# Attention scores of three of four attentions in three float32r products instead of one float32 product

## The chip, the core and the metric

The kernel runs on one core of one Trainium2 chip. The metric is the device time of one execution in microseconds (us), from start to end. The engines are called PE (TensorE, matmul), PEld (its weight loads), DVE (VectorE), ACT (ScalarE), POOL (GpSimd) and SP (SyncE).

## What is computed

The reference is a first block (a bidirectional mLSTM with a Fourier branch and a mixture of 16 experts) followed by two attention layers. Each layer has two attentions over 1,024 tokens, so there are four, called A, B, C and D here. The change touches A, B and D. Their scores are the part that matters:

```python
# A: differential attention, 4 heads with two 64-wide halves each
s = jnp.einsum("bqhcd,bkhcd->bhcqk", qb, k) * scale
s = s - (slopes[:, None, None] * dist)[None, :, None]
s = jnp.where(allowed, s, -jnp.inf); p = jax.nn.softmax(s, axis=-1)
w = p[:, :, 0] - lam * p[:, :, 1]
o = jnp.einsum("bhqk,bkhe->bqhe", w, v)       # then an RMS norm per row
# B: forgetting attention, 8 heads of 64, causal
s = jnp.einsum("bqhd,bkhd->bhqk", qb, k) * scale + cq[..., :, None] - cum[:, :, None, :]
# D: 8 heads of 64, each chunk of 64 queries sees 9 chunks of keys
s = jnp.einsum("bnqhd,bnkhd->bnhqk", qc, kb) * scale + bias[None, None]
```

## The kernel before

The program is written by hand in Bass: every engine has its own list of instructions, each runs strictly in the order in which it was written, and semaphores tie the lists together. The second block runs in stages: projections of queries and keys (`qk_pe` and its kin), the projection of the values, the attention, and so on for A, B, gates and output, then C, D, gates and output.

`Attn` holds the plan of an attention. There are 32 pairs of (c, b): c is one of four columns of heads (a head with two halves for A, two heads for the others), b is a block of 128 queries. Within a c the blocks come in the order 7, 0, 6, 1, 5, 2, 4, 3. A pair covers nk blocks of 128 keys; in A and B that is b + 1, so 8, 1, 7, 2, 6, 3, 5, 4, and in D at most 5, so 5, 1, 5, 2, 5, 3, 5, 4. Scores of a pair are made in chunks of up to 512 keys, one or two per pair; each attention has 48 chunks. By width, A and B have 24 of 512, 8 of 384, 8 of 256 and 8 of 128 columns each; D has 20, 4, 4 and 20.

A chunk is two float32 matmuls that contract over 64 rows each: half 0 on rows 0 to 63, half 1 on rows 64 to 127 (line 1591). The trace shows each float32 matmul as two records, so a chunk is four. The stationary operand is the block of queries, the moving one the keys.

All engines go through the same steps i. In step i with pair a = i:
- PE: scores(a, chunk 0), transposes of pair i-3 for half 0, scores(a, chunk 1), the product with the values of pair i-4 (`outputs`), transposes for half 1. Chunk q of the scores waits until DVE has read chunk q-2, since there are two sets of banks.
- DVE: `maxima(a, 0)` (line 2686: adds the bias, finds the row maxima, and moves the scores from PSUM), `weights(i-2)`, `empty(i-3)` (line 2721), `maxima(a, 1)`, `outputs(i-4)` (line 2732 in A, 2735 otherwise), and in A at the end of a column `complete` (lines 2740 and 2742), which waits for ACT's square root.
- ACT: exponentials of pair i-1 for half 0 (line 2078), emptying of the transposes of pair i-3 (line 2090), exponentials for half 1, and in A, one step before DVE's `complete`, `squares(c)` (line 2098 and the root on line 2101). That step is i = 11, 19, 27 and 35.

The biases are strips of 512 KB that POOL loads by DMA into a few regions in turn (`BIAS`, lines 497 to 499 and 1076 to 1086). The load into a region that was used waits until the last column that reads it has been through `maxima`. B has eight strips, one for each head; column c reads strips 2c and 2c+1.

`S` gives a semaphore, `before` the count that earlier stages left on a shared one. `split[...]` are float32r views of the same memory.

Of the kernel before, what the change touches and what calls it, by code (L numbers as in the profile page):

```python
# [53 lines left out]
class Attn:  # L54
# [5 lines left out]
    def __init__(self, p, layer, mix0, span, dv):  # L60
        self.p, self.layer, self.mix0, self.dv = p, layer, mix0, dv
        self.heads = 1 if p == "A" else 2
        blocks = [b for i in range(TT // 2) for b in (TT - 1 - i, i)]
        self.pairs = [(c, b, max(0, b - span), b - max(0, b - span) + 1) for c in range(4) for b in blocks]
        self.n = len(self.pairs)
        self.chunks = [(q[3] + 3) // 4 for q in self.pairs]
        self.chunk0 = [sum(self.chunks[:g]) for g in range(self.n + 1)]
        self.last = {q[0]: g for g, q in enumerate(self.pairs)}
        self.fins = {}
        if p == "A":  # L70
            for c in range(4):
# [8 lines left out]
        self.wide0 = [sum(1 for o in self.order[:i] if wide(o)) for i in range(len(self.order) + 1)]  # L80

    def bias_uses(self, c):
# [14 lines left out]
def build(nc, a, out, scratch):  # L97
# [21 lines left out]
    with ctx:  # L119
# [12 lines left out]
        def before(name):  # L132
# [9 lines left out]
                       for p in ("aq", "ak", "bq", "bk", "cq", "ck", "dq", "dk")])  # L142
# [3 lines left out]
                        ("x2_in", {str(3 + i): 16 for i in range(3)})])  # L146
        share("gpsimd", [("mirror", {"ed": 4}), ("gain", {"ed": TT}), ("r0norm", {"ed": 4}), ("r1norm", {"ed": 16})])
        share("few", [(p, {"_mm": 1}) for p in ("gate", "mid", "dn", "forget")])
        share("dram", [(p, {"_out": 16, "_in": 16}) for p in ("hT", "fu")])
# [7 lines left out]
                            "_pv": at.n, "_o": at.n, "_on": 4 if n == "A" else 0,  # L157
                            **{"A": {"_bias0": 32, "_bias1": 32}, "B": {f"_bias{i}": 32 for i in range(4)},
                               "C": {"_bias0": 16}, "D": {f"_bias{i}": 32 for i in range(4)}}[n]})
                       for n, at in ATT.items()])  # L160

        def sb(name, cols, dt=F32, parts=P):
# [10 lines left out]
                   ("kctx", NH * CTX), ("cols", NCH * 4 * NG),  # L173
                   ("sel_wT", 8 * P), ("lam_f", 448), ("dftc", 2 * P + 1))
        with ExitStack() as views:
            split = {n: views.enter_context(nc.sbuf_tensor(n + "_r", [P, c], F32R)) for n, c in REGIONS}
        ring, hidden, ctx_hidden, pair, wide, small, kctx, cols, sel_wT, lam_f, dftc = (sb(n, c) for n, c in REGIONS)
        ident = sb("ident", P)
# [12 lines left out]
        wrt = sb("wrt", KT * NEXP)  # L191
        extra = sb("extra", SEQ)
        wgate = extra[:, 0:KT * (FROW + NG)]
# [276 lines left out]
        def aff_slot(t):  # L470
# [674 lines left out]
        def _(pe):  # L1145
# [432 lines left out]
            def attn_pe(name):  # L1578
# [3 lines left out]
                def scores(g, j):  # L1582
# [155 lines left out]
        def _(act):  # L1738
# [272 lines left out]
            def qk_act(*keys, then_v=None, norm=None, root=None, stats=None, aside=None, late=None):  # L2011
# [33 lines left out]
                if then_v:  # L2045
                    for t in range(TT):
                        next_job(s2, len(items) + t, every, src)
                        if then_v == "dv" and t == 0:
                            act.wait_ge(S("rC_out"), before("rC_out") + 16)
# [19 lines left out]
            def attn_act(name):  # L2069
# [39 lines left out]
                for i, (a, e, _, t, u, fins) in enumerate(at.steps()):  # L2109
# [124 lines left out]
        def _(dve):  # L2234
# [373 lines left out]
            def qk_dve(*keys, then_v=None, norm=None, norms=None, sums=None, aside=None, late=None):  # L2608
# [33 lines left out]
                if then_v:  # L2642
                    for t in range(TT):
                        next_job(s2, len(items) + t, every, src)
                        if then_v == "dv" and t == 0:
                            dve.wait_ge(S("rC_out"), before("rC_out") + 16)
# [13 lines left out]
            def attn_dve(name):  # L2660
# [94 lines left out]
                for i, (a, _, w, t, u, fins) in enumerate(at.steps()):  # L2755
# [16 lines left out]
                    for c in fins:  # L2772
                        mix(c)

            def gates_dve(layer):
# [198 lines left out]
```

## Time and profile before

| | |
|---|---|
| median of 3 runs | 3056.41 us (3053.8 to 3064.21) |
| span of the profiled execution | 3053.8 us |
| attention A | about 1797 to 1926 us of the span |
| attention B | about 2096 to 2226 us |
| attention D | about 2736 to 2846 us |
| PE busy | 2816.0 us (92%) |
| DVE busy | 1606.6 us (53%) |
| ACT busy | 1331.7 us (44%) |

Busy time is the union of the instructions' spans. Matmuls are pipelined, and their records overlap, so how long a matmul holds PE is read from the distance of two starts and not from a record's own duration. An idle time in square brackets names the engine that ended it.

### The profile page before, as it was taken

The page shows a single profiled execution, that of the slowest core. Times are in us where ns is not written, and L with a number is a line of the kernel's source. Part 1 is how long each engine was busy: PE and PEld are TensorE (multiplying, and loading weights), DVE is VectorE, ACT ScalarE, POOL GpSimd, SP SyncE. Part 2 cuts the span into 40 slices and gives each one's busy share as a digit, 9 for nine tenths or more (in the row PEclk, how much of TensorE's full clock was granted, in tenths as well). Part 3 has the DMA queues.
Part 4 walks back from the last instruction along what each step waited for, and adds up shares of the span by engine and source line. Part 5 has one row for each costly group of instructions (what it writes and reads, how often), then busy time and mean ns, then how long its engine had stood idle before and what let it go on. Part 6 is the DMA issues. An engine that isn't in the chain of part 4 may idle for free. (4 is left out here: it accounts for less than half of the span.)

```text
span 3053.8 us, 37726 instructions
## 1 busy us (share of the span) xinstructions
PE 2816.0 (92%) x13816; PEld 2062.0 (68%) x13830; DVE 1606.6 (53%) x3074; ACT 1331.7 (44%) x2473; POOL 215.5 (7%) x248
## 2 busy tenths in 40 slices
PE   6899999999994899999997998999999989999998
PEld 3457885788783666666665765676677775866676
DVE  1258553344357666666645558554632556536533
ACT  2333253232242555555535537644642548437421
POOL 0000000000000011100005000000020000000500
PEclk9999999999995999999998999999999999999999
DMA  9510020323424799999975300201042201000321
GB/s 363 193 55 28 28 84 1 110 83 110 154 104 179 266 360 362 365 364 363 362 249 142 83 21 8 56 29 42 15 119 75 97 15 57 28 18 19 111 83 55
DMA packets 178377, 401.25 MB, mean 131 GB/s; under 512 B 7948, under 2 KB 9004, under 8 KB 177712
## 3 DMA queue, kind: packets, MB, share of 16 engines
q1 hardware_dynamic: 158224, 329.27, 30.7%
q0 software_dynamic: 19856, 69.92, 7.0%
q8 instruction: 97, 1.59, 0.2%
q14 instruction: 56, 0.46, 0.0%
q10 hardware_dynamic: 144, 0.01, 0.0%
HBM read 363.37 MB, written 35.81 MB: 131 GB/s over the span
## 5 line engine op out<-in xcount | busy, mean ns | idle before, releaser
L778 PE MATMUL psum<-ring_r,kctx_r 128*128 128x512 f32 (+1 forms) x544 | 213.9, 393 | 0.0
L778 PE MATMUL psum<-ring_r,cols_r 128*128 128x512 f32 (+1 forms) x544 | 213.4, 392 | 0.0
L2078 ACT ACTIVATE ring<-ring,att 128x256 f32<-128x256 f32 (+7 forms) x256 | 173.2, 677 | 68.5 <-DVE att L2686 68.5
L1591 PE MATMUL psum<-wide 64*128 64x512 f32 (+2 forms) x704 | 149.7, 505 | 17.1 <-DVE att L2686 14.2
L2549 DVE TENSOR_TENSOR ring_r<-ring,pair_r 128x1024 fp32r<-128x1024 f32 x128 | 148.0, 1218 | 21.6 <-ACT pair_r L1965 21.6
L1462 PE MATMUL psum<-ring_r,wide_r 128*128 128x512 f32 x384 | 150.3, 391 | 0.0
L616 DVE TENSOR_TENSOR ring_r<-ring,ring_r 128x1024 fp32r<-128x1024 f32 x48 | 58.7, 1225 | 129.7 <-ACT ring_r L613 129.3
L1404 PE MATMUL psum<-small_r,ring_r 128*128 128x512 f32 x320 | 125.8, 393 | 0.8 <-DVE pair L2439 0.8
L1406 PE MATMUL psum<-small_r,ring_r 128*128 128x512 f32 x320 | 126.3, 395 | 0.0
L1965 ACT ACTIVATE pair_r<-ring 128x1024 fp32r<-128x1024 f32 x128 | 124.4, 1046 | 0.0
L778 PEld LDWEIGHTS psum<-ring_r,kctx_r 128*128 128x128 f32 x544 | 105.1, 193 | 22.4
L1609 PE MATMUL psum<-ident,ring 128*128 128x128 f32 x640 | 116.9, 291 | 1.6 <-DVE ring L2713 1.6
L778 PEld LDWEIGHTS psum<-ring_r,cols_r 128*128 128x128 f32 x544 | 103.7, 191 | 21.6
L1609 PEld LDWEIGHTS psum<-ident,ring 128*128 128x128 f32 x640 | 67.9, 141 | 73.8 <-issue 40.0
L777 PE MATMUL psum<-small_r,kctx_r 128*128 128x512 f32 (+1 forms) x240 | 100.8, 420 | 18.3 <-DVE sel_wT_r L746 9.0
L300 PE MATMUL psum<-pair,wide 128*128 128x512 f32 x256 | 114.1, 599 | 2.9 <-DMA pair<-in_w_down 2.9
L300 PE MATMUL psum<-hidden,wide 128*128 128x512 f32 x256 | 112.6, 593 | 1.0 <-DVE wide L2560 1.0
L777 PE MATMUL psum<-small_r,cols_r 128*128 128x512 f32 (+1 forms) x240 | 98.7, 411 | 15.4 <-DVE wide_r L746 14.1
L1461 PE MATMUL psum<-pair_r,wide_r 128*128 128x512 f32 x256 | 101.9, 398 | 4.5 <-DVE ring_r L2549 3.1
L1405 PE MATMUL psum<-hidden_r,ring_r 128*128 128x512 f32 x256 | 101.1, 395 | 0.0
L1696 PE MATMUL psum<-wide_r,ring_r 128*128 128x512 f32 x256 | 100.6, 393 | 0.0
L1463 PE MATMUL psum<-pair_r,wide_r 128*128 128x512 f32 x256 | 100.4, 392 | 0.0
(542 smaller groups left out, 6976.3 us busy)
## 6 DMA issues: line engine op xcount, KB each, us to landing
ring<-in_w_gate SPq DMA_DIRECT2D x64, 1024.0 KB, 8.8
ring<-in_w_up SPq DMA_DIRECT2D x32, 1024.0 KB, 9.5
hidden<-in_w_up SPq DMA_DIRECT2D x32, 1024.0 KB, 9.4
hidden<-in_w_down SPq DMA_DIRECT2D x32, 1024.0 KB, 7.2
pair<-in_w_down SPq DMA_DIRECT2D x32, 1024.0 KB, 8.8
ring<-in_w_ada SPq DMA_DIRECT2D x24, 1024.0 KB, 13.1
ring<-in_w_in SPq DMA_DIRECT2D x24, 1024.0 KB, 7.1
ring<-in_even_w_in SPq DMA_DIRECT2D x16, 1024.0 KB, 13.8
```

Of the source, the lines that this page charges most:

```text
L300: mm = pe.matmul(outp, l, r, start=(i == 0), stop=(i == len(pairs) - 1))
L777: self.eng.matmul(outp, XHIGH[b][:, k, :], whigh(key, k)[:, 0:wd], start=(k == 0), stop=False)
L778: self.eng.matmul(outp, XHIGH[b][:, k, :], low[:, k, 0:wd], start=False, stop=False)
L1404: pe.matmul(outp, w, high[:, j, :], start=(j == 0), stop=False)
L1406: mm = pe.matmul(outp, lows[:, k, span(c)], high[:, j, :], start=False, stop=(j == kn - 1))
L1461: pe.matmul(outp, xh[:, k, :], high, start=(k == 0), stop=False)
L1462: pe.matmul(outp, xh[:, k, :], low[:, k, :], start=False, stop=False)
L1591: mm = pe.matmul(bank(2 * (q % 2) + h)[:, 0:n], qT2[row, c, span(b)], kT2[row, 0 if name == "C" else c, k:k + n], start=True, stop=not dia ...
L1609: mm = pe.transpose(turned(i)[:, span(k)], sv[:, span(k)], ident[:])
L1965: act.activation(MHIGH[j % 2][p // 2][:, PK * (p % 2):PK * (p % 2 + 1), :], MRAW[slot][:, ks, :], ACT.Copy).then_inc(S("mw_high"), 1)
L2078: act.activation(sv, sv, ACT.Exp, bias=nmx[:, q:q + 1], scale=-1.0, accum_out=esum[:, r:r + 1]).then_inc(S(name + "_e"), 1)
L2549: dve.tensor_tensor(MLOW[slot][:, ks, :], MRAW[slot][:, ks, :], MHIGH[j % 2][p // 2][:, PK * (p % 2):PK * (p % 2 + 1), :].bitcast(F32), AL ...
```

## The change

For A, B and D each key and query vector is split on chip: ACT copies it, rounded to float32r, to a "high" region (`split_high`), and DVE subtracts the high part from it and writes the remainder over the original, as float32r (`split_low`). The scores become three float32r products in place of one float32 product: high x high, high x low of the keys, low of the queries x high. Each of them is again done on the two row halves. C keeps its float32 product.

Keys are split a column at a time (128x1024). Queries are split a column at a time in A (128x1024) and a block at a time in B and D (128x128). The first ones (`ahead`) are split in the projection of the values, at t = 2. The others are at the end of a step's work, behind everything else of that step: after the pairs 3, 11 and 19 the next column's keys (in A the queries too), and in B and D in each of the first 29 steps the queries of the pair three steps on. On DVE a `split_low` waits for the `split_high` of the same piece. PE waits before a pair's first chunk for its `split_low`.

The region `extra` is now needed for the keys' high part. So B's biases have three regions in turn and not four, and D's third bias region is in `ctx_hidden`.

```diff
+        per = self.n // 4
+        self.ahead = [("k", 0), ("q", 0)] if p == "A" else [("k", 0)] + [("q", g) for g in range(3)]
+        self.splits, self.split_of, made = {}, {}, list(self.ahead)
+        for i in range(self.n):
+            self.splits[i] = [("k", i // per + 1)] if i % per == 3 and i // per < 3 else []
+            if p == "A":
+                self.splits[i] += [("q", c) for _, c in self.splits[i]]
+            elif i + 3 < self.n:
+                self.splits[i].append(("q", i + 3))
...
-        BIAS = {"A": [cols[:, 0:D], extra[:]], "B": [cols[:, 0:D], extra[:], tail, ctx_hidden[:, 0:D]],
+        BIAS = {"A": [cols[:, 0:D], extra[:]], "B": [cols[:, 0:D], tail, ctx_hidden[:, 0:D]],
                 "C": [ctx_hidden[:, i * 256:(i + 1) * 256] for i in range(8)],
-                "D": [cols[:, 0:640], cols[:, 640:1280], extra[:, 0:640], tail[:, 0:640]]}
+                "D": [cols[:, 0:640], cols[:, 640:1280], ctx_hidden[:, 0:640], tail[:, 0:640]]}
...
+        def split_high(act, name, event):
...
+            src, high, _ = halves_of(name, event)
+            act.activation(high, src, ACT.Copy).then_inc(S(name + "_high"), 1)
+
+        def split_low(eng, name, event):
+
+            eng.wait_ge(S(name + "_high"), before(name + "_high") + ATT[name].split_of[event] + 1)
+            src, high, low = halves_of(name, event)
+            eng.tensor_tensor(low, src, high.bitcast(F32), ALU.subtract).then_inc(S(name + "_low"), 1)
...
-                    for h in range(2):
-                        row = slice(HD * h, HD * (h + 1))
-                        mm = pe.matmul(bank(2 * (q % 2) + h)[:, 0:n], qT2[row, c, span(b)], kT2[row, 0 if name == "C" else c, k:k + n],
-                                       start=True, stop=not diagonal, skip_group_check=diagonal)
+                    if name == "C":
+                        factors = [(qT2[:, c, span(b)], kT2[:, 0, k:k + n])]
+                    else:
+                        if j == 0:
+                            pe.wait_ge(S(name + "_low"), before(name + "_low") + at.split_before(g))
+                        qh, kh = QHIGH[name][c % 2][:, span(b)] if name == "A" else QHIGH[name][g % 4], KHIGH[name][c % 2][:, k:k + n]
+                        factors = [(qh, kh), (qh, klow[:, c, k:k + n]), (qlow[:, c, span(b)], kh)]
+                    for f, (qf, kf) in enumerate(factors):
+                        for h in range(2):
...
                     for c in fins:
                         mix(c)
+                    if name != "C" and a is not None:
+                        for event in at.splits[a]:
+                            split_high(act, name, event)
...
+                    if name != "C" and a is not None:
+                        for event in at.splits[a]:
+                            split_low(dve, name, event)
```

On ACT in attention A, at the end of step 11 (line 2098 are the squares, 2101 their root, 2078 the exponentials, 2090 the emptied transposes). Before:

```order
L2090 ACTIVATE kctx<-psum 128x512
L2078 ACTIVATE ring,att<-ring,att 128x896
L2098 ACTIVATE cols,qst<-small 128x128 x8
L2101 ACT_TABLE_LOAD
L2101 ACTIVATE qst<-qst,epsc 128x8
L2078 ACT_TABLE_LOAD
L2078 ACTIVATE ring,att<-ring,att 128x256
```

After (2163, 2166, 2143 and 2155 are the same four lines, 543 is `split_high`):

```order
L2155 ACTIVATE kctx<-psum 128x512
L2143 ACTIVATE ring,att<-ring,att 128x896
L2163 ACTIVATE cols,qst<-small 128x128 x8
L2166 ACT_TABLE_LOAD
L2166 ACTIVATE qst<-qst,epsc 128x8
L543 ACTIVATE hidden_r<-wide 128x1024 x2
L2143 ACT_TABLE_LOAD
L2143 ACTIVATE ring,att<-ring,att 128x256
```

The two high copies stand behind the squares and the root, ahead of the next exponentials.

On DVE at the same place (2713 weights, 2721 emptied transposes, 2732 outputs, 2686 the maxima of step 12). Before:

```order
L2713 SCALAR_TENSOR_TENSOR ring<-ring,att 128x128
L2721 COPY kctx<-psum 128x512
L2732 TENSOR_SCALAR small<-psum,att 128x128
L2686 ISA ring,att<-psum,extra 128x512
L2686 ISA att 128x1
```

After (2784, 2792, 2803 and 2757 are the same lines, 549 is `split_low`):

```order
L2784 SCALAR_TENSOR_TENSOR ring<-ring,att 128x128
L2792 COPY kctx<-psum 128x512
L2803 TENSOR_SCALAR small<-psum,att 128x128
L549 TENSOR_TENSOR wide_r<-wide,hidden_r 128x1024 x2
L2757 ISA ring,att<-psum,extra 128x512
L2757 ISA att 128x1
```

The two low parts stand between the outputs of step 11 and the maxima of step 12.

On PE in attention A, step 4 (1591 scores, 1609 a transpose, 1629 values). Before:

```order
L1591 MATMUL psum<-wide 128x512 x2
L1609 MATMUL psum<-ident,ring 128x128
L1591 MATMUL psum<-wide 128x256 x2
L1629 MATMUL psum<-small,kctx 128x128 x8
```

After (1649 scores, 1667 a transpose, 1687 values):

```order
L1649 MATMUL psum<-hidden_r 128x512 x2
L1649 MATMUL psum<-wide_r,hidden_r 128x512 x2
L1649 MATMUL psum<-hidden_r,wide_r 128x512 x2
L1667 MATMUL psum<-ident,ring 128x128
L1649 MATMUL psum<-hidden_r 128x256 x2
L1649 MATMUL psum<-wide_r,hidden_r 128x256 x2
L1649 MATMUL psum<-hidden_r,wide_r 128x256 x2
L1687 MATMUL psum<-small,kctx 128x128 x8
```

Each chunk has three pairs of matmuls in place of one; nothing else moves on PE.

## Rows read from the trace of the kernel before

**Rows 1.** The page: its first line.

```profile
span 3053.8 us, 37726 instructions
```

**Rows 2.** Busy time by stretch (us, busy by engine): one column of A, B, D.

```profile
1837.80:1869.60 31.80, 27.48 (x167) 17.87 (x165) 28.02 (x95) 22.78 (x60) 0.53 (x1) 0.95 0.05 18
...
2137.80:2169.00 31.20, 31.10 (x282) 19.70 (x282) 19.12 (x72) 19.88 (x49) 1.05 (x2) 1.00 0.11 35
...
2750.10:2775.40 25.30, 25.30 (x230) 16.13 (x226) 15.40 (x71) 18.53 (x51) 1.07 (x2) 1.00 0.08 28
```

**Rows 3.** Timeline of DVE in A, steps 11 to 13 (start us, us, what).

```profile
1837.48 0.34 DVE L2732 TENSOR_SCALAR small<-psum,att 128x128 f32<-128x128 f32 x1
1837.99 0.69 DVE L2686 CUSTOM_DVE_ANT_0 ring<-psum,extra 128x512 f32<-128x512 f32 x1 [0.17 <-issue]
...
1842.95 0.20 DVE L2740 RECIPROCAL qst<-qst 128x8 f32<-128x8 f32 x1 [1.01 <-ACT qst L2101]
...
1844.76 0.55 DVE L2686 CUSTOM_DVE_ANT_0 ring<-psum,extra 128x384 f32<-128x384 f32 x1
```

**Rows 4.** Timeline of ACT at the same place.

```profile
1837.86 0.31 ACT L2098 ACTIVATE cols<-small 128x128 f32<-128x128 f32 x1 [0.47 <-DVE small L2732]
...
1842.62 0.30 ACT L2101 ACTIVATE qst<-qst,epsc 128x8 f32<-128x8 f32 x1
```

**Rows 5.** Timeline of ACT and of DVE in A between steps 3 and 4.

```profile
1812.00 0.50 ACT L2078 ACTIVATE ring<-ring,att 128x256 f32<-128x256 f32 x1
```

```profile
1811.94 0.68 DVE L2686 CUSTOM_DVE_ANT_0 ring<-psum,cols 128x512 f32<-128x512 f32 x1
```

**Rows 6.** Timeline of ACT and of DVE: high and low parts of a weight tile.

```profile
1984.67 1.99 ACT L757 ACTIVATE small_r<-ring 128x1024 fp32r<-128x1024 f32 x2
```

```profile
1986.45 2.35 DVE L760 TENSOR_TENSOR ring_r<-ring,small_r 128x1024 fp32r<-128x1024 f32 x2
```

**Rows 7.** Timeline of DVE in A, step 16.

```profile
1851.86 0.69 DVE L2686 CUSTOM_DVE_ANT_0 ring<-psum,extra 128x512 f32<-128x512 f32 x1 [0.81 <-PE psum L1591]
```

**Rows 8.** Timeline of PE in D, steps 12 and 13.

```profile
2775.39 1.13 PE L1591 MATMUL psum<-wide 64*128 64x512 f32 x4
2776.45 0.33 PE L1609 MATMUL psum<-ident,ring 128*128 128x128 f32 x1
2776.71 0.49 PE L1591 MATMUL psum<-wide 64*128 64x128 f32 x4
2777.13 0.32 PE L1633 MATMUL psum<-kctx,small 128*64 128x128 f32 x1
...
2778.63 0.92 PE L1591 MATMUL psum<-wide 64*128 64x384 f32 x4
2779.48 0.66 PE L1609 MATMUL psum<-ident,ring 128*128 128x128 f32 x4
```

**Rows 9.** Timeline of PE in projections: float32r products, 512 and 256 columns.

```profile
1736.31 0.39 PE L778 MATMUL psum<-ring_r,kctx_r 128*128 128x512 f32 x1
1736.53 0.39 PE L779 MATMUL psum<-small_r,sel_wT_r 128*128 128x512 f32 x1
```

```profile
2486.02 0.28 PE L778 MATMUL psum<-ring_r,cols_r 128*128 128x256 f32 x1
2486.14 0.28 PE L779 MATMUL psum<-small_r,wide_r 128*128 128x256 f32 x1
```

**Rows 10.** B, first to second column: POOL's load, its landing (KB, us), DVE.

```profile
2121.44 0.53 POOL L1084 DMA_DIRECT2D cols<-scratch_ncum  x1 [30.35 <-DVE att L2686]
```

```profile
cols<-scratch_ncum POOLq DMA_DIRECT2D x1, 512.0 KB, 4.1
```

```profile
2123.85 0.69 DVE L2686 CUSTOM_DVE_ANT_0 ring<-psum,ctx_hidden 128x512 f32<-128x512 f32 x1
```

**Rows 11.** Timeline of ACT and of DVE in D between steps 11 and 12.

```profile
2775.39 0.60 ACT L2090 ACTIVATE sel_wT<-psum 128x512 f32<-128x512 f32 x1 [0.24 <-PE psum L1609]
```

```profile
2777.28 0.69 DVE L2686 CUSTOM_DVE_ANT_0 ring<-psum,wide 128x512 f32<-128x512 f32 x1
```

More of the change, by code:

```diff
@@ L80, in __init__, with split_before @@
         self.wide0 = [sum(1 for o in self.order[:i] if wide(o)) for i in range(len(self.order) + 1)]
+        per = self.n // 4
[7 more added lines that the diff above has]
+                self.splits[i].append(("q", i + 3))
+            made += self.splits[i]
+        self.split_of = {e: i for i, e in enumerate(made)}
+    def split_before(self, g):
+        c = self.pairs[g][0]
+        return max(self.split_of["k", c], self.split_of["q", c if self.p == "A" else g]) + 1
     def bias_uses(self, c):
@@ L147, in build @@
         share("gpsimd", [("mirror", {"ed": 4}), ("gain", {"ed": TT}), ("r0norm", {"ed": 4}), ("r1norm", {"ed": 16})])
+        share("ready", [("hm_mm", {"": TT}), ("A_high", {"": 8}), ("B_high", {"": 36}), ("D_high", {"": 36})])
+        share("taken", [("hm_ev", {"": TT}), ("A_low", {"": 8}), ("B_low", {"": 36}), ("D_low", {"": 36})])
         share("few", [(p, {"_mm": 1}) for p in ("gate", "mid", "dn", "forget")])
@@ L191, in build @@
         wrt = sb("wrt", KT * NEXP)
-        extra = sb("extra", SEQ)
         wgate = extra[:, 0:KT * (FROW + NG)]
@@ new lines, in build @@
+        late_k, late_q = [split["extra"], split["ctx_hidden"][:, D:2 * D]], [split["small"][:, OB0 + 2 * D:OB0 + 2 * D + P], split["small"][:, OB0 + 2 * D + P:OB0 + 2 * D + 2 * P],
+                                                                    split["dftc"][:, 0:P], split["dftc"][:, P:2 * P]]
+        KHIGH = {"A": [split["hidden"][:, (4 + i) * D:(5 + i) * D] for i in range(2)], "B": late_k, "D": late_k}
+        QHIGH = {"A": [split["hidden"][:, (6 + i) * D:(7 + i) * D] for i in range(2)], "B": late_q, "D": late_q}
@@ new lines, in build, with halves_of @@
+        qlow, klow = (split["wide"][:, i * 4 * D:(i + 1) * 4 * D].rearrange("p (c n) -> p c n", c=4) for i in range(2))
+        def halves_of(name, event):
+            kind, i = event
+            if kind == "k":
+                return kT2[:, i, :], KHIGH[name][i % 2][:, 0:SEQ], klow[:, i, :]
+            if name == "A":
+                return qT2[:, i, :], QHIGH[name][i % 2], qlow[:, i, :]
+            c, b = ATT[name].pairs[i][0:2]
+            return qT2[:, c, span(b)], QHIGH[name][i % 4], qlow[:, c, span(b)]
@@ new lines, in split_high @@
+        def split_high(act, name, event):
+            at, (kind, i) = ATT[name], event
+            if kind == "k" or name == "A":
+                ended = 8 * (i - 1) if i >= 2 else 0
+            else:
+                ended = i - 3 if i >= 4 else 0
+            if ended:
+                act.wait_ge(S(name + "_qk"), before(name + "_qk") + at.chunk0[ended])
+            src, high, _ = halves_of(name, event)
[4 more added lines that the diff above has]
+            eng.tensor_tensor(low, src, high.bitcast(F32), ALU.subtract).then_inc(S(name + "_low"), 1)
@@ L1588, in scores @@
                     k = (k0 + 4 * j) * P
-                    for h in range(2):
-                        row = slice(HD * h, HD * (h + 1))
-                        mm = pe.matmul(bank(2 * (q % 2) + h)[:, 0:n], qT2[row, c, span(b)], kT2[row, 0 if name == "C" else c, k:k + n],
-                                       start=True, stop=not diagonal, skip_group_check=diagonal)
+                    if name == "C":
+                        factors = [(qT2[:, c, span(b)], kT2[:, 0, k:k + n])]
+                    else:
+                        if j == 0:
[4 more added lines that the diff above has]
+                        for h in range(2):
+                            row, last = slice(HD * h, HD * (h + 1)), f + 1 == len(factors)
+                            mm = pe.matmul(bank(2 * (q % 2) + h)[:, 0:n], qf[row, :], kf[row, :], start=(f == 0), stop=last and not diagonal,
+                                           skip_group_check=True)
                     if diagonal:
@@ L2047, in qk_act @@
                         next_job(s2, len(items) + t, every, src)
+                        if t == 2:
+                            for key in keys:
+                                act.wait_ge(S(key + "_evA"), before(key + "_evA") + TT)
+                            if then_v == "av":
+                                act.wait_ge(S("res0_out"), before("res0_out") + 16 * TT)
+                            for event in ATT[then_v[0].upper()].ahead:
+                                split_high(act, then_v[0].upper(), event)
                         if then_v == "dv" and t == 0:
@@ L2644, in qk_dve @@
                         next_job(s2, len(items) + t, every, src)
+                        if t == 2:
+                            for event in ATT[then_v[0].upper()].ahead:
+                                split_low(dve, then_v[0].upper(), event)
                         if then_v == "dv" and t == 0:
```

6 lines of the change are left out of this document (3 added, 3 removed).

## The prediction, made before the changed kernel ran

> **What bounds the kernel now.** I read the table of busy time by stretch first, one column of heads for each attention, because the change touches these three stages alone. In B and D PE is busy 31.10 of 31.20 us and 25.30 of 25.30 us, and DVE and ACT under two thirds [rows 2]: there PE's own time sets the pace. A is different. A column takes 31.80 us, PE is busy 27.48 of it, DVE 28.02 [rows 2], and on DVE's timeline instruction follows instruction nearly without a gap: of its 3.8 idle us in a column 1.0 is a wait for ACT's root [rows 3], 0.81 the longest wait for PE [rows 7], and the rest is short. So A runs at DVE's pace. The timelines of DVE and ACT, read side by side at the steps at which the new instructions stand, then say what the new waits cost.
>
> **PE: the chunks.** A float32 chunk holds PE for 1.06 us at 512 columns, 0.85 at 384 and 0.42 at 128, from its start to that of the next instruction [rows 8]. That is 0.213 us for each 128 columns and 0.21 fixed, which I take as two weight loads that nothing covers, the chunk's first and the next instruction's, about 0.105 each. A float32r product starts 0.22 to 0.24 us after the one before at 512 columns, 0.232 in the mean, and 0.12 after at 256 [rows 9]. A new chunk is two such distances, one product's own streaming (0.053 us for each 128 columns) and the fixed 0.21: 0.89 at 512, 0.73 at 384 (distance 0.175, between the two measured), 0.56 at 256. The savings are 0.17, 0.12 and 0.08 (256 before: 0.635). No row has a float32r product of 128 columns. Below, its distance can't be under a weight load (0.105), which gives 0.48, a loss of 0.06; above, I bound it by the 512-column distance, which gives 0.21 + 3 x 0.23 = 0.90, a loss of 0.48. I take 0.06, since the distance fell from 0.232 to 0.12 when the columns were halved, down to about a load.
>
> A column of B saves 6 x 0.17 + 2 x 0.12 + 2 x 0.08 - 2 x 0.06 = 1.3 us, B 5.2. A column of D saves 5 x 0.17 + 0.12 + 0.08 - 5 x 0.06 = 0.75, D 3.0. In both the first three or four steps are not paced by PE but by the first bias load and the filled pipeline; I take off 0.8 us each: 4.4 and 2.2.
>
> That the two halves of a float32r product run side by side, as the two float32 halves do, is taken from the float32 rows.
> The Trainium skill's page "TensorE: Matmul & The Clock Gate", in its part on packing small matmuls ("The mechanism"), says that a weight load overlaps a running matmul only if it is for another row group. By that rule each chunk would have its three loads bare, some 0.2 us more than my chunk, and the saving at 512 columns would be gone. The float32 chunk speaks against it: its 1.06 us have room for only one bare load before four passes, though it has two records for each half.
>
> **A: the new waits on DVE.** After step 11, DVE's outputs end at 1837.8 and the maxima of step 12 start at 1837.99 [rows 3]. Now the two low parts come between, each waiting for its high part on ACT. But ACT goes from 1837.86 through squares, table load and root until 1842.92 [rows 4], and only then makes the high parts. A 128x1024 high part is 1.0 us (two in 1.99), a low part 1.2 (two in 2.35) [rows 6]. So high keys are ready at about 1843.95, high queries at 1845.0; DVE does low keys from 1844.0 and is through with the queries at 1846.4. Then comes step 12's work of 3.96 us (1837.99 to the idle second ahead of 1842.95 [rows 3]), to 1850.4, and `complete` at once, 1.8 us (1842.95 to 1844.76 [rows 3]), to 1852.2. Before, step 13 started at 1844.76 [rows 3]. The delay is 7.4 us. Step 19 has the same instructions in the same order: 7.4 again. After step 3 there are no squares: ACT is free at 1812.0, DVE at 1811.94 [rows 5]; DVE waits 1.1, works 2.4: 3.5 us. Together 18.3.
>
> What gives some back: the waits of DVE for PE in the three later columns, at most 3.8 - 1.0 = 2.8 us each [rows 2, 3], the longest 0.81 [rows 7]. They shrink by up to 0.17 for each chunk ahead of them, and partly because PE has caught up. I take 2.3 us off in all (ends 0.5 and 4.5): A is 16.0 longer, 14 to 18. PE's savings in A are otherwise worth nothing, as PE is not late there.
>
> **B: bias and splits.** With three regions, strip 3 can be loaded only when column 0 has left the region of strip 0. POOL's load starts at 2121.44 and lands 4.1 us later, at 2125.6; the strip is wanted at 2123.85 [rows 10]. Before, that strip had a fourth region and was long there. DVE waits 1.7 us, the same at strips 5 and 7. DVE is idle 12 of 31 us [rows 2], so most is caught up before PE needs it; I take 0.5 each, ends 0 and 1.7. The keys' split after steps 3, 11 and 19 puts back the maxima of the next step by about 1.6 us, just as long as PE can do without: 0.2 each. The block splits of the queries, an eighth as wide as the pieces of rows 6 and so some 0.3 us on each engine, 8 in a column, fall in waits of both: 11 idle us of ACT and 12 of DVE in 31 [rows 2]. B: -4.4 + 1.5 + 0.6 = -2.3 (ends -4.4 and +1.3).
>
> **D: the keys' split bites.** After step 11 ACT's emptying starts at 2775.39 and gives way at 2775.9 [rows 11]; high keys until 2776.95, low keys from 2777.0 to 2778.15, low queries to 2778.4, then the maxima of step 12 for two halves of 0.69 each to 2779.75 (now the second starts at 2777.28 [rows 11]). PE's 384-column scores of step 13, which wait for these maxima, start at 2778.63 now [rows 8], and could at 2778.5. They wait 1.25 us, and the late DVE costs a little more at the next wide transposes: 1.4 each, 4.2 for three (ends 1 and 6). In B the same step of PE has the values of eight blocks and not five, so PE comes later and there is no such wait. D: -2.2 + 4.2 = +2.0.
>
> The first splits, in the values' projection, I cost at nothing: PE sets the pace there with products 0.23 us apart [rows 9], 24 to a job, so 5.6 us, against which ACT has one 1.0 and DVE one 1.2 us piece of rows, made before the splits. POOL's stores, which ACT now waits for in A's, are long done. If that cover failed, it would be 3.5 us for each stage.
>
> **Sum.** 16.0 - 2.3 + 2.0 = +15.7 us. The profiled execution spans 3053.8 us [rows 1], the lowest of the three runs; the median is 2.6 higher. 3056.4 + 15.7 = 3072.
>
> **Rivals.**
> 1. Narrow float32r products are dear: 0.90 us a chunk, 0.42 over my price for 8 chunks in B and 20 in D: +12, 3084. For it: no row has one. Against: the fall from 512 to 256 columns.
> 2. The halves don't run side by side, or the loads lie bare. With six distances in a row, a 512-column chunk is 0.21 + 6 x 0.22 = 1.5, B and D some 20 us longer each: 3115; with bare loads only (the page's rule) 96 chunks by 0.2, 3091. Against: the float32 rows.
> 3. The wait for ACT in A is absent or covered, and only DVE's work is added, 3 x 2.4 less 2: A +5, 3061. It would need the high parts to be made before the squares; ACT's order says otherwise.
> 4. Faster: PE, not DVE, paces A (it is busy 27.48 us of a column, nearly as long as DVE [rows 2]). Then A saves 5 us too, and DVE's late low parts are made good in its idle time: -5 - 4.4 - 2.2, 3045. It decides if the idle time of DVE in a column exceeds what is added; that is 3.8 us against 7.4.
>
> **How the numbers follow.** Forecast 0.60, rival 1 0.15, rival 2 0.08, rival 3 0.10, rival 4 0.07. The range reaches from below rival 3 to above rival 1: 3058 to 3088. 0.3% (9 us, about what a measurement of this kernel can tell from no change) is at 3047 and 3066. Slower: four fifths of the forecast, rivals 1 and 2: 0.71. Same: the rest of the forecast, rival 3: 0.21. Faster: 0.08.
>
> **What would show it.** In the changed profile: in A, DVE idle for about 6 us ahead of the first low part at steps 11 and 19, ended by ACT's copy on line 543, and for 1.1 at step 3; A some 16 us longer. Score chunks of 0.89 us at 512 columns and near 0.48 at 128 in B and D. In B, DVE waiting 1.7 us for a bias DMA three times. In D, PE waiting over a microsecond ahead of the 384-column scores. It is wrong if A grows by less than 10 us, or if a 128-column chunk takes 0.6 or more.

## The result

| | before | changed |
|---|---|---|
| median | 3057.84 us (3053.8 to 3064.21, 4 runs) | 3074.74 us (3073.2 to 3081.44, 4 runs) |
| span of the profiled execution | 3053.8 us | 3071.8 us |
| A, start of the first maxima to end of the last | 114.2 us | 135.2 us |
| B, likewise | 121.2 us | 118.5 us |
| D, likewise | 100.1 us | 102.4 us |

The ratio is 1.0052, with a 95% interval from 1.0039 to 1.0066: slower by 16.9 us by the medians, 12 to 20 by the interval, where +15.7 was forecast. The spans differ by 18.0 us. Of these, -2.9 had come about before A began, in work that the change doesn't touch; A gives +21.0, B -2.7, D +2.3, and the stretches between and behind them the rest.

The page of the changed kernel begins:

```profile
span 3071.8 us, 38561 instructions
```

Busy time by stretch, the same views as [rows 2], of one column from step 12 (A) and steps 11 (B, D) on. The columns are the stretch, its length, busy us of PE, PEld, DVE, ACT and POOL, then the granted clock, DMA share and GB/s.

```profile
1849.10:1887.80 38.70, 27.69 (x188) 21.50 (x188) 30.16 (x97) 24.98 (x62) 0.53 (x1) 0.85 0.05 15
2153.00:2183.25 30.25, 29.89 (x306) 21.61 (x305) 21.57 (x83) 22.23 (x58) 1.05 (x2) 1.00 0.11 37
2791.30:2817.50 26.20, 25.14 (x254) 18.16 (x252) 18.68 (x82) 20.91 (x58) 1.07 (x2) 1.00 0.08 27
```

In A a column now takes 38.7 us and neither engine fills it: PE 27.7, DVE 30.2. The hole is a wait. DVE and ACT at the end of step 11, where [rows 3, 4] stood (549 is `split_low`, 543 `split_high`, 2757 the maxima, 2803 the outputs, 2163 and 2166 squares and root):

```profile
1840.47 0.34 DVE L2803 TENSOR_SCALAR small<-psum,att 128x128 f32<-128x128 f32 x1
1846.87 2.36 DVE L549 TENSOR_TENSOR wide_r<-wide,hidden_r 128x1024 fp32r<-128x1024 f32 x2 [6.06 <-ACT hidden_r L543]
1849.15 0.68 DVE L2757 CUSTOM_DVE_ANT_0 ring<-psum,extra 128x512 f32<-128x512 f32 x1
```

```profile
1840.84 0.31 ACT L2163 ACTIVATE cols<-small 128x128 f32<-128x128 f32 x1 [0.47 <-DVE small L2803]
...
1845.59 0.30 ACT L2166 ACTIVATE qst<-qst,epsc 128x8 f32<-128x8 f32 x1
1845.80 1.99 ACT L543 ACTIVATE hidden_r<-wide 128x1024 fp32r<-128x1024 f32 x2
```

DVE stands still for 6.06 us while ACT does eight squares, a table load and a root, and only then the high parts. After step 3, where there are no squares, the same row of DVE carries only 1.05 us:

```profile
1812.81 2.36 DVE L549 TENSOR_TENSOR wide_r<-wide,hidden_r 128x1024 fp32r<-128x1024 f32 x2 [1.05 <-ACT hidden_r L543]
```

PE in D, steps 12 and 13, the counterpart of [rows 8] (1649 scores, 1667 a transpose, 1691 values):

```profile
2793.16 0.50 PE L1649 MATMUL psum<-ctx_hidden_r,small_r 64*128 64x512 f32 x2
2793.49 0.40 PE L1649 MATMUL psum<-wide_r,small_r 64*128 64x512 f32 x2
2793.73 0.40 PE L1649 MATMUL psum<-ctx_hidden_r,wide_r 64*128 64x512 f32 x2
2794.05 0.33 PE L1667 MATMUL psum<-ident,ring 128*128 128x128 f32 x1
2794.31 0.33 PE L1649 MATMUL psum<-ctx_hidden_r,small_r 64*128 64x128 f32 x2
...
2794.79 0.32 PE L1691 MATMUL psum<-kctx,small 128*64 128x128 f32 x1
...
2797.43 0.44 PE L1649 MATMUL psum<-ctx_hidden_r,small_r 64*128 64x384 f32 x2 [1.06 <-DVE att L2757]
...
2798.16 0.66 PE L1667 MATMUL psum<-ident,ring 128*128 128x128 f32 x4
```

From the first start to that of the next instruction, a chunk takes 2794.05 - 2793.16 = 0.89 us at 512 columns, 2794.79 - 2794.31 = 0.48 at 128 and 2798.16 - 2797.43 = 0.73 at 384. Ahead of the 384-column scores PE waits 1.06 us for DVE's maxima. What makes DVE late is one row further up, on DVE in D:

```profile
2794.73 1.22 DVE L549 TENSOR_TENSOR wide_r<-wide,extra_r 128x1024 fp32r<-128x1024 f32 x1 [1.18 <-ACT extra_r L543]
```

In B, POOL's load and the maxima that wait for it, first to second column, against [rows 10]:

```profile
2139.04 0.53 POOL L1134 DMA_DIRECT2D cols<-scratch_ncum  x1 [30.41 <-DVE att L2757]
```

```profile
2143.59 0.69 DVE L2757 CUSTOM_DVE_ANT_0 ring<-psum,cols 128x512 f32<-128x512 f32 x1 [2.22 <-DMA cols<-scratch_ncum]
```

The table that the rest leans on is made of the starts of the first maxima of each step in A: their distances in us, for the profiled execution of each kernel. Steps not shown agree within 0.25 us in all of these.

| step of A | before | changed | a_high_first | a_low_pool | a_fillers | a_float32 | best | best_fillers |
|---|---|---|---|---|---|---|---|---|
| 1 | 1.69 | 3.68 | 3.68 | 3.68 | 1.59 | 4.00 | 1.69 | 1.69 |
| 2 | 4.18 | 4.86 | 4.66 | 4.59 | 4.07 | 4.72 | 4.18 | 4.18 |
| 3 | 2.07 | 5.47 | 4.33 | 2.06 | 5.48 | 2.07 | 2.07 | 2.07 |
| 6 | 3.46 | 3.46 | 3.46 | 3.46 | 5.58 | 3.46 | 3.46 | 3.46 |
| 11 | 2.56 | 10.74 | 4.59 | 4.23 | 10.74 | 2.56 | 2.56 | 2.56 |
| 12 | 6.77 | 5.66 | 5.66 | 7.02 | 5.66 | 6.77 | 6.77 | 6.78 |
| 14 | 4.51 | 4.72 | 5.06 | 5.73 | 4.70 | 4.78 | 4.52 | 3.46 |
| 19 | 2.56 | 10.74 | 4.58 | 4.23 | 10.74 | 2.56 | 2.56 | 2.56 |
| 20 | 6.77 | 5.66 | 5.66 | 7.01 | 5.66 | 6.77 | 6.78 | 6.77 |
| 21 | 3.17 | 2.59 | 2.59 | 2.80 | 2.59 | 2.73 | 3.23 | 2.58 |
| 22 | 3.95 | 3.46 | 5.60 | 5.53 | 5.93 | 4.39 | 5.37 | 3.46 |
| 29 | 2.59 | 2.59 | 2.59 | 2.59 | 2.58 | 3.23 | 2.71 | 2.59 |
| 30 | 3.46 | 5.93 | 4.67 | 5.94 | 3.46 | 5.26 | 4.40 | 3.46 |

Two kinds of steps are in it. Steps 3, 11, 12, 19 and 20 give the same number in every execution with the same instructions. The others take two or more values in kernels whose instructions there are the same: a_float32 has in A exactly the instructions of the kernel before, and takes 4.00 us for step 1 and 5.26 for step 30 where the profiled run before took 1.69 and 3.46. There the granted clock of PE differs, as shown under a_fillers and best_fillers.

### The profile page after: what moved, and what is told of

It is laid out like the page before. It is cut to its first block and busy times, and to the rows that moved or that the text cites. A ratio compares the mean times of both kernels' runs of the same rounds, so it can differ in the third digit from the quotient of the medians.

```text
span 3071.8 us, 38561 instructions
## 1 busy us (share of the span) xinstructions
PE 2814.9 (92%) x14104; PEld 2091.3 (68%) x14118; DVE 1641.8 (53%) x3154; ACT 1358.5 (44%) x2553; POOL 215.8 (7%) x248
## 5 line engine op out<-in xcount | busy, mean ns | idle before, releaser
L829 PE MATMUL psum<-small_r,sel_wT_r 128*128 128x512 f32 (+1 forms) x240 | 96.4, 402 | 0.0
```

The source lines that it names most:

```text
L829: mm = self.eng.matmul(outp, XLOW[b][:, k, :], whigh(key, k)[:, 0:wd], start=False, stop=(k == KT - 1))
```

## Experiments

All times are compared with the kernel before on the same chip; its medians there were 3059.6 to 3060.7 us. Each kernel is the changed one with the edit shown.

**The high parts ahead of the squares.** ACT's loop, one step's start in place of its end, for A:

```diff
+                    if name == "A" and a is not None:
+                        for event in at.splits[a]:
+                            split_high(act, name, event)
                     if e is not None:
                         exponentials(e, (0,))
...
-                    if name != "C" and a is not None:
+                    if name in ("B", "D") and a is not None:
```

> In A, ACT makes the high parts of the next column at the start of steps 3, 11 and 19, ahead of the exponentials and so ahead of the squares and the root. DVE's low parts stay where they are. If the queue behind the squares is what A pays for, DVE's idle time of 1.05 + 6.06 + 6.06 = 13.2 us ahead of the low parts goes to nothing, DVE's waits of 1 us for the root at steps 12 and 20 come back, and A (first to last maxima, 135.2 us) falls by some 11 us to 124; the kernel takes about 3063.5 us. If it is DVE's own work on the low parts (2.4 us three times) or PE that paces A, the idle time only moves and A stays above 132 us.

Measured: 3063.86 us, ratio 1.0013 (1.0003 to 1.0022); A 122.8 us. DVE at step 11 (here 2806 are the outputs, 2760 the maxima):

```profile
1839.85 0.34 DVE L2806 TENSOR_SCALAR small<-psum,att 128x128 f32<-128x128 f32 x1
1840.11 2.35 DVE L549 TENSOR_TENSOR wide_r<-wide,hidden_r 128x1024 fp32r<-128x1024 f32 x2
1842.38 0.68 DVE L2760 CUSTOM_DVE_ANT_0 ring<-psum,extra 128x512 f32<-128x512 f32 x1
```

The instructions are the same, and the wait is gone. Steps 3, 11 and 19 fall by 1.1, 6.15 and 6.16 us. So 13.4 us of A are DVE's wait for the high parts: 12.3 of them at steps 11 and 19, where they stand behind the squares, the table load and the root, and 1.1 at step 3, where they stand behind ACT's other work alone. What stays is 2.0 to 2.3 us a step, DVE's own work. Steps 12 and 20 don't go back to 6.77: the 2.4 us of low parts lie where DVE waited for the root before, so that wait of 1.1 us is paid for by them.

**A in float32, B and D split.**

```diff
-                    if name == "C":
-                        factors = [(qT2[:, c, span(b)], kT2[:, 0, k:k + n])]
+                    if name in ("A", "C"):
+                        factors = [(qT2[:, c, span(b)], kT2[:, 0 if name == "C" else c, k:k + n])]
```

(and no splits for A on either engine.)

> A alone is put back: float32 scores and no splits; B and D keep their three products. A goes back to 114.2 us from 135.2. If B and D together are worth nothing, as their stages say (-2.7 and +2.3 us), the kernel takes what it took before the change, 3058 us within 2. If the gain from narrow PE chunks were larger and hidden in the comparison, it would be under 3053; if B and D carried a loss that the stages don't show, above 3062.

Measured: 3060.96 us, ratio 1.0005 (0.9995 to 1.0015). B takes 118.7 and D 102.1 us, as in the changed kernel. So A is the whole loss, 1.0052 less 1.0005 or some 14 us (9 to 20, if the two intervals are put together), and B and D together are worth nothing that can be measured. A itself took 119.8 us and not 114.2, with the same instructions: PE's granted clock over A was 0.91 in this profile and 0.97 in the one before.

**The keys' high part a step early in B and D.**

```diff
                         for event in at.splits[a]:
-                            split_high(act, name, event)
+                            if name == "A" or event[0] == "q":
+                                split_high(act, name, event)
+                        if name != "A" and a % 8 == 2 and a // 8 < 3:
+                            split_high(act, name, ("k", a // 8 + 1))
```

> In B and D, ACT makes the keys' high part one step earlier (end of steps 2, 10, 18) and DVE's low part stays at the end of steps 3, 11 and 19. If D's stall is DVE waiting for ACT (1.18 us ahead of the low keys at step 11), that idle time goes, PE's waits ahead of the 384-column scores (1.46, 1.07, 1.07 us) fall under 0.3 each, and D, 102.4 us, gets 2.5 to 3.5 shorter; B changes by less than 0.3, since PE doesn't wait there: 3072. If DVE's work of 1.5 us is what makes PE late, PE still waits 0.7 or more each time and D gets less than 1.2 shorter.

Measured: 3073.38 us, ratio 1.0043 (1.0028 to 1.0057); D 98.9 us, B 118.7. PE in D at the place shown above:

```profile
2800.00 0.33 PE L1667 MATMUL psum<-ident,ring 128*128 128x128 f32 x1
2800.41 0.44 PE L1649 MATMUL psum<-ctx_hidden_r,small_r 64*128 64x384 f32 x2
```

The wait of 1.06 us is gone, and steps 3 to 5, 11 to 13 and 19 to 21 of D are 1.53, 1.00 and 1.00 us shorter, 3.5 in all. It was DVE's wait for ACT, not its work. B didn't notice (10.98 us for steps 11 to 13 in both).

**Four bias regions in B.**

```diff
-"B": [cols[:, 0:D], tail, ctx_hidden[:, 0:D]],
+"B": [hidden[:, 7 * D:8 * D], cols[:, 0:D], tail, ctx_hidden[:, 0:D]],
```

> B's biases have four regions again: the fourth is the part of the hidden region that B's own column 3 fills last. DVE's waits of 2.2, 1.8 and 1.7 us for the bias loads of strips 3, 5 and 7 go. If they cost what the stage shows at steps 9, 17 and 25 (1.0, 0.55 and 0.5 us), B falls by 1.5 to 2.1 us from 118.5. If DVE's idle time covers them all, B stays within 0.3 us.

Measured: 3074.98 us, ratio 1.0049 (1.0032 to 1.0065); the time doesn't tell it from the changed kernel. B takes 117.1 us, 1.4 less, by column: the second 29.93 us (30.72 in the changed kernel), the third 29.93 (30.26), the last seven steps 26.67 (26.97). With three regions the wait also varies, since the load does. In a_high_first one strip took 6.1 us to land and not 4.1:

```profile
2161.96 0.69 DVE L2760 CUSTOM_DVE_ANT_0 ring<-psum,ctx_hidden 128x512 f32<-128x512 f32 x1 [3.78 <-DMA ctx_hidden<-scratch_ncum]
```

There B's third column took 33.76 us, 3.8 more than with four regions. In the changed kernel waits of 2.2, 1.8 and 1.7 us cost B 0.8, 0.3 and 0.3, so DVE's idle time covered some 1.4 us of each. By that count the wait of 3.78 us would cost 2.4, and it cost all of it. PE's granted clock was also down, to 0.76 over the 7 us behind this wait; whether that is the difference was not tested.

**A's low parts on POOL**, on top of a_high_first:

```diff
                             pool.dma_start(o, a["strip_a"][i]).then_inc(S(f"A_bias{i % nb}"), 16)
+                            if 1 <= i:
+                                for event in at.splits[8 * i - 5]:
+                                    split_low(pool, "A", event)
```

> As a_high_first, and POOL makes A's low parts of columns 1 to 3, so that DVE is free of them. If DVE's own work on them is what was left (its steps 3, 11 and 19 still take 4.33, 4.59 and 4.58 us from maxima to maxima, before the change 2.07, 2.56 and 2.56), they fall to the old values, A loses 6.3 us, and the kernel takes 3057.5 us (from 3063.9). If POOL is too slow for the next step's scores, or slows DVE while it works, the three steps keep over half of the 6.3 us.

Measured: 3064.71 us, ratio 1.0010 (0.9999 to 1.0021), no better than a_high_first. Step 3 fell to its old 2.06 us, but steps 11 and 19 only to 4.23, and 12 and 20 rose. POOL, and DVE beside it (2790 is `weights`):

```profile
1838.54 5.08 POOL L549 TENSOR_TENSOR wide_r<-wide,hidden_r 128x1024 fp32r<-128x1024 f32 x2 [9.48 <-ACT hidden_r L543]
```

```profile
1841.51 2.26 DVE L2790 SCALAR_TENSOR_TENSOR ring<-ring,att 128x128 f32<-128x128 f32 x1
1843.70 0.68 DVE L2798 COPY kctx<-psum 128x512 f32<-128x512 f32 x1
```

The same 128x128 instruction takes 0.35 us in a_high_first:

```profile
1838.98 0.35 DVE L2787 SCALAR_TENSOR_TENSOR ring<-ring,att 128x128 f32<-128x128 f32 x1
```

It ends at 1843.78, 0.15 us after POOL. The maxima, which ran beside POOL at 1840.3 and read PSUM, kept their 0.42 us. So this DVE instruction, which reads two operands from SBUF, stood still while POOL did such work itself. The Trainium skill, "SBUF — State Buffer", section "SBUF: two separate sides", says that DVE and GpSimd share one pair of ports, held exclusively for a whole instruction; the trace agrees, with 1.9 us of blocking.

**The same, two steps earlier** (in steps 1, 9 and 17 in place of 3, 11 and 19; a column's keys are first used at steps 8, 16 and 24, so seven steps ahead and not ten), and with the edits of best for B and D:

```diff
-            self.splits[i] = [("k", i // per + 1)] if i % per == 3 and i // per < 3 else []
+            self.splits[i] = [("k", i // per + 1)] if i % per == (1 if p == "A" else 3) and i // per < 3 else []
```

> As best, but A has the three products too, with the high parts made by ACT at the start of steps 1, 9 and 17 and the low parts by POOL right after them (two in 5.1 us, as measured in a_low_pool), ten steps' work ahead of their use. If DVE is A's bound and PE's saving is worth nothing there, steps 3, 11 and 19 take 2.1, 2.4 to 2.6 and 2.4 to 2.6 us, A is within 1.5 us of float32's but for steps 1, 6, 14, 22, 29 and 30, where PE's clock moves it, and the kernel is within 2 us of best, 3052.3. If PE's saving were worth its 1.3 us per column in A, A would be 4 us shorter and the kernel at 3048.

Measured: 3057.59 us, ratio 0.9991 (0.9981 to 1.0), 5.3 us above best, not within 2. Steps 11 and 19 take 2.82 and 2.81 us, near the old value of 2.56, as POOL no longer works beside them. But the steps in which it does, 9 and 17, take 3.98 and 4.10 us where best has 2.34, and step 30, one of those that follow the clock, takes 5.88. The `weights` of step 9, 0.75 us in best:

```profile
1831.91 2.67 DVE L2793 SCALAR_TENSOR_TENSOR ring<-ring,att 128x512 f32<-128x512 f32 x1
```

The same instruction is held up again, by 1.9 us: POOL is no second DVE for this work. In A the three products bring 0.17 us in each of steps 15, 23, 25 and 27 and no more, even with the splits off DVE.

**Fillers for the clock, changed kernel.**

```diff
+                    if name == "A" and i == 0:
+                        filler(10, bank(6))
+                    if name == "A" and i == 29:
+                        pe.wait_ge(S("A_o"), before("A_o") + u)
+                        filler(10, bank(6))
                     if u is not None:
                         outputs(u)
```

> The changed kernel with ten more filler matmuls (bf16, 512 columns, results unused) in A at step 0, while PE waits for the first maxima, and ten at step 29, while it waits for the last transposes. If step 1 (3.7 us in the changed kernel and 1.7 in the profiled run before) and step 30 (5.9 and 3.5) are long because PE's granted clock falls to 0.5 after it stood idle for about 3 us, it stays at 1.0 there, step 1 takes 1.7 to 2.2 and step 30 3.5 to 4 us, and A falls by 3 to 4 us. If they are long because of the split scores themselves, both keep their length, or get longer by the fillers.

Measured: 3076.12 us, ratio 1.0047 (1.0029 to 1.0065). Steps 1 and 30 were 1.59 and 3.46 us, as the clock theory has it. Two stretches of the changed kernel, after PE stood idle for 3.1 and 2.9 us:

```profile
1799.80:1803.00 3.20, 2.80 (x12) 1.35 (x13) 1.78 (x10) 2.48 (x5) 0.00 (x0) 0.50 0.00 0
1924.00:1932.30 8.30, 7.78 (x37) 5.76 (x38) 5.97 (x21) 5.33 (x15) 0.00 (x0) 0.60 0.00 1
```

In a_fillers the second place (steps 29 and 30) shows 1.00:

```profile
1926.00:1936.00 10.00, 8.83 (x61) 5.80 (x61) 8.65 (x32) 8.99 (x24) 0.00 (x0) 1.00 0.00 1
```

But A was 134.6 us, only 0.6 less, since steps 6 and 22 were now 2.1 and 2.5 us longer: PE still stood idle for 2.4 to 7 us behind the splits, and its clock was 0.50 there. Step 1 was short in halves_in_turn too, without a filler. This run alone settles nothing.

**The halves in turn.**

```diff
-                    for f, (qf, kf) in enumerate(factors):
-                        for h in range(2):
+                    for h in range(2):
+                        for f, (qf, kf) in enumerate(factors):
```

> The six products of a chunk in another order: the three of half 0 first, then the three of half 1. If products run side by side only where neighbours in the queue use different row halves, just one of three pairs is left, a 512-column chunk takes 0.21 + 5 x 0.23 = 1.36 us in place of 0.89, B and D get 13 to 20 us longer each, and A some too. If each product's place in the queue doesn't matter, chunk and stages stay as they are.

Measured: 3075.11 us, ratio 1.0049 (1.0030 to 1.0068): the rival was right. PE in D, the 512-column chunk:

```profile
2794.90 0.50 PE L1649 MATMUL psum<-ctx_hidden_r,small_r 64*128 64x512 f32 x2
2795.24 0.40 PE L1649 MATMUL psum<-wide_r,small_r 64*128 64x512 f32 x2
2795.47 0.40 PE L1649 MATMUL psum<-ctx_hidden_r,wide_r 64*128 64x512 f32 x2
2795.81 0.33 PE L1667 MATMUL psum<-ident,ring 128*128 128x128 f32 x1
```

Each row still holds both halves (x2), although the program has all three products of half 0 ahead of the first of half 1. The two stand 0.01 us apart in the trace. The chunk takes 0.91 us and D's undisturbed columns 0.1 more.

**The gains together.** A in float32, the keys' high part early, four regions in B: the edits of a_float32, key_high_early and b_four_regions.

> A in float32 as before the change; B and D in three products, the keys' high part one step early, and four bias regions in B. From the stages of the single edits: B 117 us or a little less (121.2 before), D 98.9 (100.1), A unchanged. So 5 us below the kernel before, ratio 0.998. If the gains don't add up, or the runs with a disturbed clock hide them, within 2 us of it.

Measured: 3052.27 us, ratio 0.9971 (0.9960 to 0.9982), faster than both kernels. That is 9 us below the kernel before (5 to 12 by the interval; the medians are 8 apart) rather than 5. B at 117.9 and D at 99.3 us account for 4 of them; nothing here shows where the rest comes from, and at the interval's lower end it is down to 1 us.

**Best with fillers in A**, ten at step 0 and ten at steps 13, 21 and 29, ahead of the outputs.

> As best, with ten unused bf16 filler matmuls of 512 columns (about 2.2 us) in A where PE stood idle for 2.56 us before the outputs of steps 13, 21 and 29, and at step 0. If PE's granted clock of 0.5 to 0.7 after these idle times costs time, steps 22 and 30 of A fall from 5.37 and 4.40 us to 3.95 and 3.46 or less, A from 116.8 to under 114, and the median by 2 to 3 us under that of best, 3052.3. If the clock falls all the same, at other places, or the fillers come late, the median stays within 1.5 us of it.

Measured: 3045.91 us, ratio 0.9960 (0.9944 to 0.9976), with a median 6 us below that of best, where 2 to 3 were expected. The two ratios, each to the kernel before on the same chip, are only 3 us apart and their intervals overlap, so the size is better read from the profile of A: 116.8 us in best and 112.1 here, 4.7 less (the other two profiles of the same A without fillers had 114.2 and 119.8). PE at step 21 in best, and the granted clock behind it:

```profile
1876.56 0.79 PE L1687 MATMUL psum<-small,sel_wT 128*128 128x128 f32 x2 [2.57 <-ACT sel_wT L2153]
```

```profile
1876.50:1880.50 4.00, 3.94 (x12) 1.79 (x12) 3.37 (x12) 3.90 (x12) 0.00 (x0) 0.50 0.00 0
```

and in best_fillers:

```profile
1873.94 0.49 PE L1687 MATMUL psum<-small,sel_wT 128*128 128x128 f32 x2 [0.41 <-ACT sel_wT L2158]
```

```profile
1873.90:1877.90 4.00, 3.79 (x25) 2.56 (x26) 3.89 (x15) 4.00 (x11) 0.00 (x0) 1.00 0.00 0
```

The same product takes 0.79 us at the lower level (1.2 GHz) and 0.49 at the higher (2.4 GHz). A is shorter than in any kernel without fillers, and its granted clock is 1.00 throughout. Steps 14, 22 and 30 are 3.46 us each, in best 4.52, 5.37 and 4.40. So it was the clock that made these steps long, and the idle time ahead of them that lowered it.

**Fillers in B and D too.**

```diff
-                    if name == "A" and i == 0:
-                        filler(10, bank(6))
+                    if i == 0 and name != "C":
+                        filler({"A": 10, "B": 15, "D": 12}[name], bank(6))
```

> As best_fillers, with fillers at step 0 of B (15) and D (12) too, where PE stands idle for 4.2 and 3.8 us while the first bias strips land, and after which its granted clock is 0.5 for the next 3.5 us in the changed kernel and in the one before alike. If that is why D's first column saves nothing by the split (steps 1 and 2 take 3.83 and 3.5 us, before the change 3.43 and 3.22), they get 0.3 to 0.8 us shorter in sum, B's steps 1 and 2 as much, and the kernel is 0.5 to 1.5 us below best_fillers, 3045.9. If D's first column is held back by DVE or by the bias load, nothing changes there.

Measured: 3042.37 us, ratio 0.9933 (0.9919 to 0.9948), the lowest median here. It is 3.5 us below that of best_fillers, where 0.5 to 1.5 were expected, and the intervals of the two ratios just overlap. B is 115.3 us, 1.7 less; its steps 1 and 2 take 2.06 and 3.89 us where they took 3.05 and 4.48. D gained nothing (99.0): twelve fillers left 2.1 us idle, and the clock was 0.50 behind them all the same. So whether the clock is what takes D's first column its gain stays untested.

## Why the prediction was right, step by step

- **What bounds each stage.** In B and D PE does, as said. In A it is DVE, but less purely than said: [rows 2] shows a granted clock of 0.95 in its column, and best_fillers takes 30.7 us for a column where the kernel before took 31.8. The 0.81 us of [rows 7], read as the longest wait for PE, end step 14 (the row is the start of step 15), and that step falls from 4.51 to 3.46 us in best_fillers: PE was at its lower clock.
- **Chunks.** Forecast 0.89, 0.73, 0.56 and 0.48 us; measured 0.89, 0.73, 0.55 and 0.48. The 128-column product, which no row showed, was near its lower bound, and rival 1 (0.90) falls. The halves run side by side and the loads lie under the matmuls, so rival 2 falls too.
- **A's stalls.** Forecast DVE idle 1.1 and twice about 6 us; measured 1.05 and twice 6.06. The delay was put at 3.5 + 7.4 + 7.4 = 18.3; the table gives 3.40 for step 3 and 8.18 - 1.11 = 7.07 for steps 11 with 12 and 19 with 20, so 17.5. Rival 3 would have needed the high parts ahead of the squares; that is a_high_first, and it gives 3064 where the rival said 3061.
- **What A gives back.** Forecast 2.3, measured 0.85 (0.17 us at steps 9, 15, 17, 23, 25 and 27, less 0.17 at step 28). That makes 16.7 for A by the steps that repeat; 16.0 was said.
- **What was missed in A.** Steps 1, 2, 14 and 30 were 5.4 us longer in the changed profile, steps 21 and 22 1.1 shorter: 4.3 in all, for PE's clock. The prediction has no such term, and A came out above its range (14 to 18, measured 21.0). The whole of A, first in the profile before and then in the changed one, the granted clock being the third number from the end:

```profile
1801.40:1915.70 114.30, 99.57 (x602) 63.02 (x603) 103.10 (x350) 80.44 (x211) 1.06 (x2) 0.97 0.03 12
```

```profile
1798.50:1933.70 135.20, 104.03 (x693) 77.29 (x695) 109.74 (x356) 86.40 (x217) 1.06 (x2) 0.86 0.03 10
```

Such steps vary between executions of the same instructions, but that doesn't make the difference chance. Three profiles have A's old instructions (before, a_float32, best): 114.2, 119.8 and 116.8 us, with a granted clock of 0.97, 0.91 and 0.94. Three have the changed ones (changed, key_high_early, b_four_regions): 135.2, 138.9 and 139.5 us, with 0.86, 0.83 and 0.82. The means lie 20.9 us apart. In the changed A PE stands idle for 7.05 us twice, at steps 12 and 20, behind the wait for the high parts, and no idle time in the old A is longer than 2.9. So part of the loss is most likely a lower clock that goes with the change. How large that part is, six profiles don't tell (halves_in_turn, with the same products in another order, had 131.4 us at 0.91), and the medians' 14 us, 9 to 20, fit 16.7 as well as 21.
- **B.** Forecast -4.4 + 1.5 + 0.6 = -2.3, measured -2.7. With four regions B saved 4.1 and a column of it 1.26 (1.3 forecast). The bias wait cost 1.4 (1.5 forecast) in this run, but up to 3.8 for one strip in another. The keys' splits cost nothing, not 0.6: steps 11 to 13, with a split, take 10.97 us, and steps 27 to 29, without one, 10.98.
- **D.** Forecast -2.2 + 4.2 = +2.0, measured +2.3, and both terms were too large. PE's waits were 1.46, 1.07 and 1.07 us, and taking them away gave 3.5 back. The saving was 1.2: 0.57 to 0.62 in a column from the second on (0.75 forecast), and the first column lost 0.6 (25.2 us in key_high_early, 24.6 before). Its step 0 was 0.64 us longer, as DVE waited 0.93 us for the second bias strip and not 0.39, and steps 1 and 2 were 0.64 longer; the other five won 0.7. In steps 1 and 2 PE's clock stayed low longer, as these stretches behind the first bias load show, first of the changed kernel and then of the one before; that this is the cause was not shown, as fillers_abd didn't lift the clock in D.

```profile
2756.50:2760.00 3.50, 3.14 (x12) 1.70 (x15) 1.61 (x10) 2.90 (x10) 0.00 (x0) 0.50 0.11 43
2760.00:2764.00 4.00, 4.00 (x20) 1.63 (x18) 1.39 (x5) 0.00 (x0) 0.00 (x0) 0.76 0.00 0
```

```profile
2740.60:2744.00 3.40, 3.02 (x10) 1.47 (x13) 1.04 (x8) 2.50 (x8) 0.00 (x0) 0.51 0.11 44
2744.00:2748.00 4.00, 4.00 (x23) 1.54 (x22) 1.69 (x8) 0.00 (x0) 0.00 (x0) 1.00 0.00 0
```

- **First splits in the values' projection.** Forecast 0. The lead or lag between the two kernels stayed within 0.2 us through the projections before A and before D.
- **Rival 4** (PE paces A) falls: nothing made A shorter than before but the clock.

So the mechanism and its place were as forecast. That the total came out within 1.2 us is partly luck: by the profiles the three stages sum to +20.6 where 15.7 was forecast, and 2.9 us of that were made up for before A, by work that the change doesn't touch. D's two terms were off in opposite directions by 1.0 and 0.7. The clock's part in A is the one piece that the prediction's steps don't hold.

## What to carry to other kernels

When an instruction is put at the end of a step, read what its supplier has queued at that moment: two copies of 1 us each behind eight squares, a table load and a root cost 6 us of the engine that set the pace, and moving them to the start of the same step gave that back. Making PE's scores cheaper in A, where PE isn't the bound, bought 0.85 us in 114, and giving DVE's low parts to POOL held up DVE, as both read two operands from SBUF. In A PE stood idle for 2.57 us in front of work that others wait for; ten unused matmuls in each such gap took 4.7 us off A, more than the cheaper products gave in B and D together.

## What the hardware showed that was not expected

- After 2.57 us idle, PE's granted clock was 0.50 for the next 4 us (best, step 21) and 1.00 when the gap was cut to 0.41 us with fillers. Over A this was worth 4.7 us by the two profiles. The Trainium skill, "TensorE: Matmul & The Clock Gate", section "What's actually happening", has the clock of an idle PE fall to 1.2 GHz; the trace agrees, with a granted clock of 0.50 behind the idle time.
- The order of the two halves' products in the queue doesn't matter: with three of half 0 ahead of three of half 1, both halves' first products start 0.01 us apart and the chunk takes 0.91 us, not 1.36. The Trainium skill, same page, section "The mechanism", says that matmuls start strictly in program order; the measurement here speaks against that for products on different row halves.
- A DVE instruction of 0.35 us took 2.26 while POOL's low part ran, and one of 0.75 took 2.67. POOL takes 2.5 us for a 128x1024 subtraction, DVE 1.2.
- A 512 KB load of a bias strip took 4.1 us in one execution and 6.1 in another, at the same place.
